# Four more stages of a float32 network: tokens turned unscaled, the norm's scale applied behind the products

## The reference, cut to what matters

```python
def rmsnorm(x, g):
    y = xf * lax.rsqrt(jnp.mean(xf * xf, axis=-1, keepdims=True) + EPS) * g
# layer 0: stick-breaking, layer 1: gating, layer 2: S5, layer 3: stick-breaking; each followed by
def conv_gated_ffn(xn, w_up, conv_w, conv_b, w_down):
    h = causal_depthwise_conv(xn @ w_up, conv_w, conv_b)      # 3 taps along the tokens
    a, g = jnp.split(h, 2, axis=-1)
    return (jax.nn.silu(g) * a) @ w_down                      # 2816 wide
def chunked_spatial_gating(xn, ...):
    u, v = jnp.split(jax.nn.gelu(xn @ w_in), 2, axis=-1) ...
def stick_breaking_attention(xn, w_qkv, w_o):                 # 16 heads of 64, q scaled by 1/8
    qkv = xn @ w_qkv ...
```

## Time and profile before

| | us |
|---|---|
| median of three runs (1660.36 to 1661.38) | 1661.0 |
| the profiled execution's own time | 1662.43 |
| its span, first to last instruction | 1660.7 |
| TensorE matmuls busy | 1626.6 (98%) |
| VectorE busy | 1193.2 (72%) |
| ScalarE busy | 926.2 (56%) |
| GpSimd busy | 340.1 (20%) |

### The profile page before, as it was taken

One profiled execution on the slowest core, in us unless ns is written; L12 is line 12 of the kernel. 1 busy time (PEld: TensorE's weight loads), 2 busy tenths in 40 slices (PEclk: granted clock), 3 DMA queues, 4 the chain that ended last, 5 costly groups with the idle time before them and its releaser, 6 DMA issues.

```text
span 1660.7 us, 28692 instructions
## 1 busy us (share of the span) xinstructions
PE 1626.6 (98%) x12208; PEld 1496.4 (90%) x12208; DVE 1193.2 (72%) x1675; ACT 926.2 (56%) x1265; POOL 340.1 (20%) x376
## 2 busy tenths in 40 slices
PE   8999999999999998999999999999999999999999
PEld 7979999898999987899998988999988898899998
DVE  5677679766786679878777676887786766665555
ACT  5665554545557768465555665555554755543444
POOL 1432799601380010000000133110007200000000
PEclk9999999999999999999999999999999999999999
DMA  7445557564556554546554534656555632555551
GB/s 247 157 147 172 181 175 244 175 201 145 194 172 203 181 182 148 179 153 203 193 188 134 171 127 154 204 177 204 177 177 155 201 105 95 168 195 178 187 192 53
DMA packets 203391, 286.12 MB, mean 172 GB/s; under 512 B 6432, under 2 KB 162272, under 8 KB 203264
## 3 DMA queue, kind: packets, MB, share of 16 engines
q1 hardware_dynamic: 197584, 272.25, 49.5%
q0 software_dynamic: 2224, 5.75, 1.4%
q10 hardware_dynamic: 3456, 6.29, 1.1%
HBM read 279.03 MB, written 5.24 MB: 171 GB/s over the span
## 4 chain that ended last, share of the span: by engine, by line
PE 85%; DVE 9%; ACT 4%; issue 1%; POOL 1%; DMA 0%; SPq 0%; DVEq 0%; ACTq 0%
PE ps L107 83%; DVE wlo L119 3%; DVE arena L119 2%; PE ps L110 2%; ACT arena L113 2%; ACT whi L113 1%; DVE ol L119 1%; DVE xres L119 1%; DVE arena L125 1%; DVE arena L122 0%; POOL sm L119 0%; DVE arena L137 0%; DVE xl L125 0%; ACT oh L113 0%; POOL arena L146 0%
## 5 line engine op out<-in xcount | busy, mean ns | idle before, releaser
L119 DVE TENSOR_TENSOR wlo<-raw,whi 128x2048 fp32r<-128x2048 f32 (+2 forms) x259 | 602.9, 2334 | 204.8 <-ACT whi L113 204.7
L107 PE MATMUL ps<-xh,whi 128*128 128x256 f32 x2296 | 655.1, 285 | 2.3 <-DVE wlo L119 1.7
L107 PE MATMUL ps<-xh,wlo 128*128 128x256 f32 x2296 | 649.5, 283 | 0.0
L107 PE MATMUL ps<-xl,whi 128*128 128x256 f32 x2296 | 649.4, 283 | 0.0
L113 ACT ACTIVATE whi<-raw 128x2048 fp32r<-128x2048 f32 (+2 forms) x259 | 490.9, 1899 | 205.8 <-PE ps L107 201.8
L107 PEld LDWEIGHTS ps<-xh,whi 128*128 128x128 f32 x2296 | 439.3, 191 | 10.0 <-issue 4.1
L107 PEld LDWEIGHTS ps<-xl,whi 128*128 128x128 f32 x2296 | 439.5, 191 | 2.0 <-issue 0.2
L107 PEld LDWEIGHTS ps<-xh,wlo 128*128 128x128 f32 x2296 | 439.4, 191 | 0.1
L107 PE MATMUL ps<-whi,oh 128*128 128x512 f32 (+1 forms) x640 | 249.3, 390 | 3.7 <-DVE ol L119 2.3
L107 PE MATMUL ps<-wlo,oh 128*128 128x512 f32 (+1 forms) x640 | 247.1, 386 | 0.0
L107 PE MATMUL ps<-whi,ol 128*128 128x512 f32 (+1 forms) x640 | 246.5, 385 | 0.0
(11 more groups left out here) (168 smaller groups left out, 1769.7 us busy)
## 6 DMA issues: line engine op xcount, KB each, us to landing
raw<-in_ffn_w_up SPq DMA_DIRECT2D x88, 1024.0 KB, 5.1
raw<-in_ffn_w_down SPq DMA_DIRECT2D x44, 1024.0 KB, 5.0
raw<-in_sb_w_qkv SPq DMA_DIRECT2D x23, 1024.0 KB, 6.8
raw<-in_w_ffn_in SPq DMA_DIRECT2D x22, 1024.0 KB, 5.0
raw<-in_w_in SPq DMA_DIRECT2D x19, 1024.0 KB, 5.2
raw<-in_w_ffn_out SPq DMA_DIRECT2D x11, 1024.0 KB, 4.8
raw<-in_sb_w_o SPq DMA_DIRECT2D x8, 1024.0 KB, 4.9
raw<-in_sg_w_in SPq DMA_DIRECT2D x8, 1024.0 KB, 5.2
```

Of the source, the lines that this page charges most:

```text
L107: return NOP if self.e is None else self.e.matmul(*a, **k)
L119: return NOP if self.e is None else self.e.tensor_tensor(*a, **k)
```

## The change

stick0, ffn0, gate and stick1 go the raw way. The diff, cut to its core ("..." marks what is left out):

```diff
-    RAW = {"ffn2": 40, "ffn3": 56, "ffn4": 72, "ple": 80}
-    RAW_AFTER = {"stick1": "ffn3", "second": "ffn4", "ffn4": "ple"}
-    RAW_BANKS = {"ffn2": (4, 5, 6, 7), "ple": (4, 6, 5, 7)}
+    RAW = {"stick0": 0, "ffn0": 8, "gate": 16, "ffn2": 40, "stick1": 48, "ffn3": 56, "ffn4": 72, "ple": 80}
+    RAW_AFTER = {"stick0": "ffn0", "ffn0": "gate", "ffn2": "stick1", "stick1": "ffn3", "second": "ffn4", "ffn4": "ple"}
+    RAW_BANKS = {"stick0": (1, 2, 3, 7), "stick1": (0, 1, 2, 3), "ffn2": (4, 5, 6, 7), "ple": (4, 6, 5, 7)}
...
+    def first_half_dve(self, dv):                 # first half of the first weight tile, high and low, on VectorE
+        raw, hi, lo = (w[0][:, 0:1024] for w in (self.raw, self.whi, self.wlo))
+        dv.wait_ge(*self.on("raw_first"))
+        dv.tensor_copy(hi, raw).then_inc(*self.up("hi_first"))
+        dv.wait_ge(*self.on("hi_first"))
+        dv.tensor_tensor(lo, raw, hi.bitcast(F32), ALU.subtract).then_inc(*self.up("lo_first"))
...
-    def up_scaled(self):
-        return carve(self.ar, 4096, 4, 256)
+    def up_scaled(self, l):
+        return carve(self.ar, 4096 if l else 8448, 4, 256)
...                                                # stick_pe
+                if st == "stick1":
+                    self.raw_turn_pe(pe, st, 0, 1)
                 ins = self.feat_major_pair(pe, w, self.qk_bank(0, 0), st)
...
+                    if (s, c, m) == (0, 1, 1):
+                        self.raw_scale_pe(pe, st)
...
-                if (blk, s, k) == (0, 0, 1):
+                if (blk, s, k) == (0, 0, 2):
                     scores(0)
...                                                # stick_act: q and k are no longer moved by ScalarE
-            if c == 0:
-                ac.activation(qT[:, 2 * s:2 * s + 2, :], bv, ACT_F.Copy, scale=0.125).then_inc(*self.up("qk_out", st, s, c))
-            else:
-                ac.activation(kT[:, 2 * s:2 * s + 2, :], bv, ACT_F.Copy).then_inc(*self.up("qk_out", st, s, c))
...                                                # stick_dve
+        def scaled(s, c):
+            bank = self.qk_bank(s, c)[:, :].rearrange("p (a b) -> p a b", b=256)
+            dv.wait_ge(*self.on("tile", "qk", st, s, c))
+            dv.wait_ge(*self.on("r_out", st))
+            if c == 0:
+                dv.scalar_tensor_tensor(qT[:, 2 * s:2 * s + 2, :], bank, SCALE, r, ALU.mult, ALU.mult).then_inc(*self.up("qk_out", st, s, c))
+            else:
+                dv.tensor_tensor(kT[:, 2 * s:2 * s + 2, :], bank, r, ALU.mult).then_inc(*self.up("qk_out", st, s, c))
...
+                if what == "qk":
+                    scaled(*key)
                 self.cut_lo(dv, (what, st) + key)
...                                                # gating_pe, first tile: the last eight transposes
+                for k in range(4):
+                    if blk == s == 0 and k in (0, 2):
+                        self.raw_turn_pe(pe, "gate", k // 2, 1)
...
-            self.out_proj_pe(pe, "gate", i, [("gu_out", 3)])
+            self.out_proj_pe(pe, "gate", i, [("u_scaled", 3), ("r_out", "gate")])
...                                                # gating_act
-            ac.wait_ge(*self.on("tile", "gu", s))
-            ac.activation(uT[:, 2 * s:2 * s + 2, :], B[4 + s % 3][:, :].rearrange("p (a b) -> p a b", b=256),
-                          ACT_F.Gelu_apprx_tanh).then_inc(*self.up("gu_out", s))
+            ac.wait_ge(*self.on("u_scaled", s))
+            ac.activation(uT[:, 2 * s:2 * s + 2, :], uT[:, 2 * s:2 * s + 2, :], ACT_F.Gelu_apprx_tanh).then_inc(*self.up("gu_out", s))
...                                                # gating_dve
+        def scaled(s):
+            dv.wait_ge(*self.on("tile", "gu", s))
+            dv.wait_ge(*self.on("r_out", "gate"))
+            dv.tensor_tensor(uT[:, 2 * s:2 * s + 2, :], self.B[4 + s % 3][:, :].rearrange("p (a b) -> p a b", b=256), r,
+                             ALU.mult).then_inc(*self.up("u_scaled", s))
+
+        self.cut_lo(dv, ("gv", 0, 1), 0)
+        self.raw_sums_dve(dv, "gate")
+        self.raw_diag_dve(dv, "gate")
...
         for g in range(8):
             middle(g)
+        scaled(2)
...
         self.cut_lo(dv, ("gu", 3))
         low(4)
         low(5)
+        scaled(3)
         product(6)
...                                                # the stage list of every engine
-        self.norm_pe(pe, "ffn0")
         self.ffn_pe(pe, 0, self.s5_prep_pe(pe, 0))
```

More of the change, by code:

```diff
@@ L371, in feat_major_pair @@
         for k in range(KT):
-            if st in self.RAW and k == 2:
+            if st in self.RAW and st != "stick0" and k == 2:
                 self.raw_turn_pe(pe, st, 1, 1)
@@ L581, in raw_scale_pe, with raw_scale_bank, raw_scale, raw_scale_act @@
             pe.wait_ge(*self.on("scaled", st, t))
-            ins = pe.matmul(self.B[3][:, t * P:(t + 1) * P], self.nones[:, :], self.diag(st)[:, t, :], start=True, stop=True)
+            ins = pe.matmul(self.raw_scale_bank(st)[:, t * P:(t + 1) * P], self.nones[:, :], self.diag(st)[:, t, :], start=True, stop=True)
         ins.then_inc(*self.up("r_turned", st))
-    def raw_scale(self):
-        return self.ar[:, 5120:5376]
+    def raw_scale_bank(self, st):
+        return self.B[7 if st == "gate" else 3]
+    def raw_scale(self, st):
+        o = {"stick0": 9984, "stick1": 9984, "ffn0": 9472, "gate": 9472}.get(st, 5120)
+        return self.ar[:, o:o + 256]
+    def raw_scale_act(self, ac, st):
+        ac.wait_ge(*self.on("r_turned", st))
+        ac.activation(self.raw_scale(st), self.raw_scale_bank(st)[:, 0:256], ACT_F.Copy).then_inc(*self.up("r_out", st))
     NORM_BANKS = {"stick0": (4, 5, 0, 1, 2, 3, 6, 7), "stick1": (4, 5, 0, 1, 2, 3, 6, 7), "s5": (4, 5, 0, 1, 2, 3, 6, 7),
@@ L1222, in gating_act @@
             ac.wait_ge(*self.on("tile", "gv", blk, 1))
+            ac.wait_ge(*self.on("r_col", "gate"))
             for t in range(2):
[L1224 removed]
+                ac.activation(vg[:, t, blk * 512:(blk + 1) * 512], B[2 * blk + t][:, :], ACT_F.Gelu_apprx_tanh,
+                              scale=self.small("rsgate", 6)[:, 4 + t:5 + t]).then_inc(*self.up("vg", blk, t))
+            if blk == 0:
+                self.raw_scale_act(ac, "gate")
         ac.wait_ge(*self.on("vg", 1, 0))
@@ L1280, in gating_dve @@
         for s in range(3):
+            if s:
+                scaled(s - 1)
             self.cut_lo(dv, ("gu", s))
@@ L3030, in scalar @@
         ac.preload_act_table_set("natural_log_exp_and_others")
-        self.norm_act(ac, "stick0", 0, more=lambda: self.cut_hi(ac, ("qk", "stick0", 0, 0), 0))
+        self.raw_act(ac, "stick0")
         self.stick_act(ac, "stick0")
-        self.norm_act(ac, "ffn0", 8)
+        self.raw_act(ac, "ffn0")
         self.ffn_act(ac, 0, self.s5_prep_act(ac, 0))
-        self.norm_act(ac, "gate", 16)
+        self.raw_act(ac, "gate")
         self.gating_act(ac)
@@ L3080, in tensor @@
         self.tiles_used = 0
-        self.norm_pe(pe, "stick0")
+        self.gains_pe(pe)
+        for j in range(2):
+            for t in range(2):
+                self.raw_turn_pe(pe, "stick0", t, j)
         self.stick_pe(pe, "stick0", self.early_pe(pe))
-        self.norm_pe(pe, "ffn0")
         self.ffn_pe(pe, 0, self.s5_prep_pe(pe, 0))
-        self.norm_pe(pe, "gate")
         self.gating_pe(pe)
```

92 lines of the change are left out of this document (52 added, 40 removed).

## The result

The changed kernel took 1691.18 us (median of 4, 1690.49 to 1692.61), against 1661.19 for the kernel before: ratio 1.0181, 95% interval 1.0169 to 1.0193. That is 30 us slower, where the prediction said +22 (1683, range 1663 to 1692). The result lies 0.8 us inside the range, and outside the 1674 to 1688 that I gave for the forecast mechanism alone. One of the eight executions of the later run with ffn0 in the scaled way took 1825.19 us at a granted clock of 0.82; it is left out of that run's time. The profiled execution took 1691.61 us with a span of 1689.9; the granted TensorE clock over it is 0.986, where it was 0.998.

The account below looks back on a forecast made before the run. TensorE, busy 98% of the span, was taken as the bound. Starts, gate's projection and ffn0's inside summed to +22.2 us on the profiled 1662.43: 1684.6, or 1683.2 against the median; range 1663 to 1692.

Parts of the forecast that it names:

- forecast mechanism alone: ffn0: VectorE and GpSimd take turns by whole instructions; 1674 to 1688 us, chance .55.
- main step: Inside ffn0: each of 13 VectorE operations a block, where it was 5, may wait for one GpSimd instruction; +25.5 us.
- Rival B: ffn0: only the first tap of a row waits for GpSimd; +6.6 us in all, 1667.6, chance .20.
- Rival C: ffn0: taps fall beside GpSimd's operations or don't wait; -0.9 us in all, 1660.1, chance .15.
- reading by shared bandwidth: ffn0: taps are slowed by at most 2.5 instead of blocked; +12.8 us, and +2.4 for scaled products, 1672.
- ffn0 term: Inside ffn0: TensorE stalls of 12.6, 7.7 and 5.7 us on `wlo`, less today's 0.5; +25.5 us.
- walk through VectorE's queue: ffn0, VectorE blocks 6 to 8 in turns with GpSimd: `wlo` done at 264.9, 289.6 and 312.3.
- gate's projection: gate's output projection waits for `u_scaled(3)` on VectorE behind `wlo`, until about 383.4 instead of 380.48; +2.9 us.
- rival D: TensorE's clock falls behind long waits, a fourth block stalls, or stick steps lack cover; +3 to +10, about 1690, chance .10.
- the stick steps: Scaled copies of q and k move to VectorE, hidden by its 1.24 us wait for `whi`; 0, uncovered 5.6 a layer.
- The starts: Raw stage starts replace the scaled ones: stick0 -1.5 us, ffn0 -2.1, gate -0.5, stick1 -2.1.

## Why the prediction held, and where its steps did not

**The main step held.** "Each of 13 operations of a block may wait for one GpSimd instruction": the taps took 1329 and 980 ns, one for one with GpSimd's operations, and either half of the condition taken away returns them to 472 or 475. Rival B (a row of taps counts as one) falls with the four-for-four rows above. Rival C (taps not hurt, 1660) falls with the taps' times. The reading by shared bandwidth (put at 1672; its terms -3.3, +12.8 and +2.4 add up to 1672.9) falls too: a tap that needs 0.3 to 0.47 alone took 1.2 beside an operation of 1.06, which is a wait for the whole of it, and 3.6 behind one of 2048 elements. The rule of the Trainium skill, "SBUF — State Buffer", section "Who interferes with whom", is that a VectorE instruction with two SBUF inputs contends with GpSimd and one with a single SBUF input does not, outside certain modes that it calls 2-port perf modes. The first part fits here, and one input in SBUF was free for the taps (472 ns beside a GpSimd that is busy all the time). I had left the condition on the modes out: the `tensor_scalar` of 128x2 has one input, in SBUF, and took 3043 ns beside GpSimd's operation of 2048 elements and 168 in the run with the lists cut. That it ran in such a mode no trace shows.

**The size of the ffn0 term was right by luck: two errors cancel.** I had +25.5, all of it waits (12.6, 7.7, 5.7 less 0.5); measured +24.4, of which the offsets jump by 10.3, 3.7 and 3.8 at the waits (17.8) and grow by 7.4 at the slow clock behind them, less 0.7 for the kernel before, whose own wait of 0.47 is gone. The walk through VectorE's queue itself was good to about 2 us: its three `wlo` ended at 264.6, 287.4 and 310.6, where I had 264.9, 289.6 and 312.3. (In the first row of taps the tiny `tensor_scalar` and three taps met GpSimd's large operations and five taps met nothing long; the 512-element list ended at 307.8, a little before my 309.) The rest of the difference is that TensorE came later than I had it: by 2.2 us at the first wait, the third block's loss, and by 2.0 at the second, with the slow clock behind the first in it.

**The clock was a term put at nothing.** I wrote that behind TensorE's waits "VectorE is the later one while that lasts, so it costs nothing". That held for 4.6 of the 9.8 us of slow time in ffn0. It failed behind the last of the waits, where VectorE has no list beside it any more (2.8), at the third block (2.4), at gate's projection (2.65), which no VectorE covers, and at stick0's start (1.5). That was rival D, at a chance of .10; its total, about 1690, is the nearest to the 1691 measured, though only a part of the 30 us is the clock's. Of D's other conditions a fourth stalled block came, but at ffn0's third block and for another cause; the stick steps had their cover.

**gate's projection.** Predicted 383.4 in old coordinates, so 3.6 of wait; it waited 4.49, 3.8 more than before. The wait was right within a microsecond. What was missing is the 2.65 of clock behind it. The run with gate's order mended shows both.

**ffn0's third block was not in the sum at all, and is the largest miss: +5.1 for 0.** The forecast followed the taps and `wlo`, but not the copy that releases the bank. With TensorE some 3 us earlier than before and two scaled products ahead of the copy, TensorE waited 3.17 in place of 0.4, and 2.4 more went to the clock. The 2.2 gained at ffn0's start was thus given back within 25 us, and more.

**The starts.** stick1 and ffn0 -2.2 each for -2.1, gate -0.8 for -0.5 with its expected wait for `wlo` (1.83 for 2.0). stick0's first product came at 11.72, 2.75 earlier, where 12.4 was forecast, but 2.46 us of idle time stood ahead of it and the clock fell to 0.50 between 14 and 16 us: 1.5 us lost, and with the scale matmuls (0.4) -0.75 in place of -1.5. In the other traces with this same start it came out between -1.0 and +0.8. The stick steps cost nothing, as forecast.

**s5.** The 1.0 that s5 takes less is clock too. Behind a wait of 2.3 us in the kernel before and 2.2 in the changed one, the slow time ends after 5.5 us and after 3.7:

```profile
656.40:661.90 5.50, 5.50 (x13) 0.50 0.97 329
```

```profile
688.66:692.40 3.74, 3.74 (x10) 0.54 0.94 335
```

It doesn't follow from a late gate: the run that is only 0.5 us late there gains the 1.0 too, and the one with gate's order mended, 24.9 us late, loses 0.3.

**What stays open.** What decides whether the clock falls behind a wait of 1.8 to 3 us. And a raw ffn0 with GpSimd's two lists moved to another stage wasn't tried; by the run with the lists cut short and gate's order mended it would be some 1667.9 - 6.0 = 1662 (an estimate): no gain over before.

## What to carry to other kernels

Before an intermediate moves from PSUM to SBUF, list the VectorE instructions that read it and count for each how many of its inputs then lie in SBUF, and look at what GpSimd does in that stretch: here eight small taps a block turned from 471 to about 1200 ns each, and a layer without that neighbour hid the same edit fully. Price a long TensorE wait with the slow time behind it (2.1 to 2.8 us here behind 3.2 to 10.1 us, less what a later engine absorbs; behind 1.83 us some 1.6 in five traces of nine), and gains at a stage's start with the next instruction that frees a bank. An instruction on which TensorE depends goes ahead of the long ones in its queue that have slack; moving two of them was worth 6 us.

## What the runs showed that was not expected

Behind waits of 3.17, 3.58, 3.59, 4.49 and 10.11 us the granted clock of the changed kernel was at 0.50 for 4.5 to 6.2 us, and the longest wait has the shortest of these stretches behind it. Over all traces it fell behind each of the eleven waits of 3.58 us and more in ffn0 and gate. Below that it is no property of the wait: the same instruction's wait of 1.83 us had it fall in five traces and not in four, and the wait at ffn0's third block had it fall behind 3.17, 3.17 and 3.18 us and not behind 3.01. Matmuls whose results nobody reads held it at 1.00 through all the waits that they filled.
